# Eight single filling places per round of a RWKV-7 chunk loop, in place of four places with six parts

## The chip, the cores and the metric

The kernel runs on one core of one Trainium2 chip. The metric is device time in microseconds (us), from the start to the end of one execution; three timed runs of the kernel before gave a median of 1094.38 us (1093.92 to 1094.64).

The core has a matrix engine (TensorE, PE in the profile; its weight loads are listed apart as PEld), a vector engine (VectorE, DVE), an activation engine (ScalarE, ACT) and GpSimd (POOL). Each runs its own instructions in the order in which they are written, and they meet at semaphores. SyncE (SP) issues the loads of the weights.

## The reference, cut to what matters

One layer of a hybrid encoder: adaLN-modulated RMSNorm, one large projection, three token mixers on its slices (differential attention, HGRN2, RWKV-7), gated merging, then a SwiGLU channel mixer. 512 tokens, width 1024, all float32. The change lies in the RWKV-7 mixer, whose recurrence is

```python
def step(state, inp):
    r_t, w_t, k_t, v_t, kk_t, a_t = inp
    sa = jnp.einsum('bhvk,bhk->bhv', state, -kk_t)
    state = (state * w_t[:, :, None, :] + sa[..., None] * (kk_t * a_t)[:, :, None, :]
             + v_t[..., None] * k_t[:, :, None, :])
    return state, jnp.einsum('bhvk,bhk->bhv', state, r_t)
```

over 8 heads of 64 by 64 state. The columns of the projection that feed the gates, HGRN2 and the attention do not depend on this recurrence.

## The kernel before

**Chunks and pairs.** The recurrence is computed in chunks of 64 tokens, two chunks (`ab` 0 and 1) to a pair, four pairs (`PAIRS`). For a pair `n`, `start_inverse(n)` (line 2414) multiplies keys by queries (`AR`, `BK`), and VectorE masks the result into `SC` (`begin_inverse`, line 1749). Then the inverse of a unit triangular 64x64 matrix per head is built in five levels. Level `i` is a chain through three engines: `level_t(n, i)` (line 2424) is 16 products of 64x64 on TensorE (`SC` by `X`), `take_t` (line 1094) copies the result from its bank to `LX` on ScalarE, `level_p(n, i)` (line 2437) is 16 more products on TensorE (`XT` by `LX`), and on VectorE `level` (line 1774) writes the result into `X` under a mask and transposes it to `XT` for the next level's `level_p`. The next level's `level_t` needs only `X`. In the last level it is `XT` that is written.

**The state.** For each chunk of pair `c`, TensorE runs `read_values` and `read_state` (right-hand side, which ScalarE copies to `rhs_u`), `out_state`, `new_values` (the inverse applied; ScalarE copies it to `UV`), `write_state` (into `M`, which VectorE adds and decays in `next_state`, line 1790) and `out_chunk`.

**The rounds.** The loop at line 2558 runs three rounds, c = 0, 1, 2. A round interleaves the state's products of pair c with the inverse of pair c + 1, so that one chain's products stand between another's. The two transposes `values_by_token` (tile `V`) and `keys_by_token` (tile `BK`) stand there too.

**Filling.** Products of the large projection are put between the small ones. A weight panel has 256 columns and is computed as two units of 128 columns, and a unit as four parts; a part is six matmuls of 128x512 (three for each of two row blocks, since each float32 operand is split into a high and a low piece). `early(place)` on TensorE (line 2262) issues as many parts as the table `EARLY` (line 64) gives that place; the count of parts over the whole RWKV stretch is fixed by the later stages. In a round there are four places: `rw lo` (two parts, behind `start_inverse`), `rw mid` (one), `rw gap` (one) and `rw hi` (two), the last three around the last two levels. So a round takes six parts, three quarters of a panel.

**What follows a place.** The functions `early` of ScalarE (line 913) and VectorE (line 1505) carry the same place names. ScalarE's copies the units that are finished out of their bank to `gate_row` and sends them to memory, and splits off the high piece of the next panel (tile `whi`); VectorE's subtracts it from the panel to get the low piece (`wlo`). Which panel is due at a place follows from the count of parts ahead of it. Both stand in their engine's order between the steps of the inverse and of the state.

**Order.** All of it is written by hand: the order in which the functions are called is the order in each engine's queue. Results of small products use four memory banks in rotation (`bank_plan`, line 202), the units two more.

Of the kernel before, what the change touches and what calls it, by code (L numbers as in the profile page):

```python
# [45 lines left out]
PAIRS = T // P  # L46
# [15 lines left out]


EARLY = [
    [("rw lora", 4), ("rw kk", 4)] + [(("rw kn", x_), 4) for x_ in range(2)]
    + [(("rw sums", n, x_), 4) for n in range(3) for x_ in range(2)]
    + [("rw pro", 4)] + [((what, i), 1) for i in range(1, 4) for what in ("rw first", "rw lev")] + [(("rw lev", 4), 2)]
    + [((what, c), n) for c in range(PAIRS - 1) for what, n in (("rw lo", 2), ("rw mid", 1), ("rw gap", 1), ("rw hi", 2))]
    + [(("rw fin", k), n) for k, n in enumerate((1, 1, 4, 2, 2))]
    + [("rw mean", 4), ("rw bv", 2), ("rw var", 2), ("rw g", 8), ("rw past", 8), ("rw end", 0)],  # L70
    [(("hg z", 0), 4), (("hg z", 1), 4)] + [(("hg sc", lev), 2) for lev in range(1, LEVELS + 1)]
# [130 lines left out]
def bank_plan():  # L202
# [78 lines left out]
    for c in range(PAIRS):  # L281
        last = c == PAIRS - 1
        b.add("rw o", c, bank=4 + c % 2)
        if last:
            two("rw r", c, 0)
            b.add("rw u", c, 0)
            b.add("rw m", c, 0)
            two("rw r", c, 1)
            b.add("rw u", c, 1)
            for _ in range(2):  # L290
                late_ada(bank=4)
            continue
        inverse_start(c + 1)
        two("rw r", c, 0)
        b.add("rw t", c + 1, 1)
        b.add("rw u", c, 0)
        level(c + 1, 1)
        b.add("rw m", c, 0)
        two("rw r", c, 1)
        b.add("rw t", c + 1, 2)  # L300
        level(c + 1, 2)
        b.add("rw u", c, 1)
        b.add("rw t", c + 1, 3)
        b.add("rw m", c, 1)
        level(c + 1, 3)
        last_levels(c + 1)
    b.rotate(6)
# [80 lines left out]
def build(nc, x, ada_w, w_in, wba, wbb, wbc, w_out, f_in, f_out, w2, a2, g2,  # L388
# [3 lines left out]
    with ExitStack() as ctx:  # L392
# [495 lines left out]
        def _(act):  # L888
# [23 lines left out]

            def early(place):

                for part in early_parts()[:stretch(place)[1]]:
                    u = evicted[0]
                    if part[1] != u or not part[5]:
                        continue
                    evicted[0] += 1
                    act.wait_ge(*full("early", u))  # L920
                    if u >= 2:
                        act.wait_ge(*spilled(u - 2))
                    do(stage[:, u % 2, :], bank_of("early", u)[:, :], ACT.Copy).then_inc(free_sem("early", u), 1)  # L923
                    act.wait_ge(*freed("early", u))
                    act.dma_start(early_out[u], stage[:, u % 2, :]).then_inc(s_spilled[u % 2], 16)
                while split_next[0] < split_by(place):
                    split_hi()
# [152 lines left out]
            act.wait_ge(s_rw_bonus_hi, up(s_rw_bonus_hi))  # L1080
            for n in range(1, 3):
                for x_ in range(2):
                    early(("rw sums", n, x_))

# [56 lines left out]
            for c in range(PAIRS - 1):  # L1141
                if c == 2:

                    act.wait_ge(s_lam_dot, 2)
                    do(col(LR, 2), col(LR, 2), ACT.Exp).then_inc(s_lam_exp, 1)
                    act.wait_ge(s_lam_exp, up(s_lam_exp))
                early(("rw lo", c))
                take_r(c, 0)
                take_t(c + 1, 1)
                take_u(c, 0)  # L1150
                take_t(c + 1, 2)
                take_r(c, 1)
                take_u(c, 1)
                take_t(c + 1, 3)
                early(("rw mid", c))
                take_t(c + 1, 4)
                if c + 2 < PAIRS:
                    take_values(c + 2)
                take_o(c)
                early(("rw gap", c))  # L1160
                early(("rw hi", c))
                take_t(c + 1, 5)
                take_keys(c + 1, 0)
                if c + 2 < PAIRS:
                    take_keys(c + 1, 1)
            c = PAIRS - 1
            early(("rw fin", 0))
            take_r(c, 0)
            early(("rw fin", 1))
            take_u(c, 0)  # L1170
# [10 lines left out]
            early("rw bv")  # L1181
            early("rw var")
            act.wait_ge(*freed("rw mean", 3))
            do(chunks(epi), O, ACT.Square).then_inc(s_rw_sq, 1)
            act.wait_ge(s_rw_sq, up(s_rw_sq))
            for c in range(4):
# [238 lines left out]
        def _(dve):  # L1425
# [280 lines left out]
            for x_ in range(2):  # L1706
                early(("rw sums", 2, x_))
            dve.wait_ge(s_rw_factor, 1)
# [64 lines left out]

            def level(n, i, state=None):

                if i < RW_LEVELS - 1:
                    dve.wait_ge(*full("rw p", n, i))
                    v.copy_predicated(X[:, :, :], lmask(i, 0), by_chunk(bank_of("rw p", n, i)[:, :]))\  # L1778
                        .then_inc(free_sem("rw p", n, i), 1)
                    dve.wait_ge(*freed("rw p", n, i))  # L1780
                    if state is not None:
                        next_state(*state)
# [25 lines left out]
            for c in range(PAIRS - 1):  # L1808
# [3 lines left out]
                elif c == 1:  # L1812
# [3 lines left out]
                    for x_ in range(2):  # L1816
# [4 lines left out]
                        dve.wait_ge(s_lam_dot, up(s_lam_dot))  # L1821
                early(("rw lo", c))
                level(c + 1, 1, (c, 0))
                level(c + 1, 2)
                next_state(c, 1)
                level(c + 1, 3)
                early(("rw mid", c))
                level(c + 1, 4)
                early(("rw gap", c))
                early(("rw hi", c))  # L1830
                level(c + 1, 5)
# [3 lines left out]
            c = PAIRS - 1  # L1835
            early(("rw fin", 0))
            early(("rw fin", 1))
            next_state(c, 0)
# [320 lines left out]
        def _(pe):  # L2159
# [225 lines left out]
            pe.wait_ge(s_rw_norm_lo, 1)  # L2385
            for c in range(4):
                ps = begin("rw kn", c)
                mm(ps[:, :], select[:, P * c:P * c + P], norm_hi[:, :], True, False)
# [7 lines left out]
            end(last, "rw bonus")  # L2396
            for x_ in range(2):
                early(("rw sums", 1, x_))
            for x_ in range(2):
                early(("rw sums", 2, x_))  # L2400

# [129 lines left out]

            def last_levels(n, fourth, between, fifth):
# [5 lines left out]
                if between:  # L2538
                    early(between)
                level_p(n, 4)  # L2540
# [10 lines left out]
            for i in range(1, 4):  # L2551
# [3 lines left out]
                if i < 3:  # L2555
                    early(("rw lev", i))
            last_levels(0, ("rw lev", 3), None, ("rw lev", 4))
            for c in range(PAIRS - 1):
                start_inverse(c + 1)
                early(("rw lo", c))  # L2560
# [44 lines left out]
            early("rw bv")  # L2605
            for c in range(4):
                ps = begin("rw bv", c)
                mm(ps[:, :], select[:, P * c:P * c + P], bonus_hi[:, :], True, False)
# [280 lines left out]
```

## Time and profile before

| | |
|---|---|
| median of three timed runs | 1094.38 us |
| the profiled execution | 1092.74 us |
| its span, first to last instruction | 1090.9 us |
| TensorE busy | 1060.5 us (97%) |
| VectorE busy | 617.5 us (57%) |
| ScalarE busy | 455.0 us (42%) |
| mean granted clock of TensorE | 0.997 of full |

The span is 1.84 us shorter than the time of the same execution, which also holds what lies around the first and the last instruction. In the timeline a row merges neighbouring instructions of one kind: its columns are the start, the duration from the first start to the last end, the engine and line, what is written from what, the tile shape, the output shape and how many instructions there are. A small float32 product is listed twice (16 products are x32). A bracket gives the engine's idle time before the row and what ended it. Matmuls overlap at their ends, so the price of a group is taken from its start to the start of the next group.

### The profile page before, as it was taken

Reading aid. Unit: us, or ns where it says so; the run is one execution under the profiler, and the core shown is the slowest. Engines: PE = TensorE matmul, PEld = TensorE weight load, DVE = VectorE, ACT = ScalarE, POOL = GpSimd, SP = SyncE. Lnnn points to the kernel's source line nnn. Section 1 sums busy time; section 2 is a strip of 40 time slices with the busy share of each in tenths; the row PEclk is TensorE's granted clock in tenths of the full one; section 3 lists DMA queues with packets and bytes.
Section 4 is the critical chain, followed back from the end, with each engine's and each line's share of the span. In section 5 each row is a group of like instructions: output and inputs, shape, how many; then the busy total and the mean of one; then the engine's idle time right before and its main releaser. Section 6 shows DMA issues by size and latency. Waiting matters only on the chain.

```text
span 1090.9 us, 17055 instructions
## 1 busy us (share of the span) xinstructions
PE 1060.5 (97%) x7093; PEld 858.2 (79%) x7093; DVE 617.5 (57%) x846; ACT 455.0 (42%) x575; POOL 26.8 (2%) x46
## 2 busy tenths in 40 slices
PE   8999999999999999999999999999999999999997
PEld 6788677788887787787667778888888888878885
DVE  3489885467535469758656388663544533242446
ACT  5422743233323476655555454581222122222233
POOL 0100001000000000020000100000000000000000
PEclk9999999999999999999999999999999999999999
DMA  9977534301107421196411485304343423222201
GB/s 341 319 243 259 173 106 140 96 14 56 54 22 260 126 96 68 48 274 229 127 57 49 149 333 187 123 20 154 116 155 116 145 87 109 85 91 103 92 25 77
DMA packets 106772, 145.29 MB, mean 133 GB/s; under 512 B 3252, under 2 KB 86440, under 8 KB 106696
## 3 DMA queue, kind: packets, MB, share of 16 engines
q1 hardware_dynamic: 93544, 109.25, 30.4%
q0 software_dynamic: 5664, 21.32, 5.9%
q10 hardware_dynamic: 7488, 13.63, 3.3%
q8 instruction: 56, 0.92, 0.3%
q14 instruction: 20, 0.16, 0.0%
HBM read 128.46 MB, written 15.73 MB: 132 GB/s over the span
## 4 chain that ended last, share of the span: by engine, by line
PE 79%; DVE 11%; ACT 5%; DMA 2%; SPq 1%; issue 1%; ACTq 0%; POOL 0%; DVEq 0%
PE bank L2178 78%; DVE Z L1430 1%; DVE wlo L1430 1%; DVE q_lev L1430 1%; DMA raw<-in_w_in 1%; DMA qk<-early_out 1%; DVE near L1922 1%; SPq L794 1%; ACT whi L908 1%; DVE SC L1430 1%; DVE mg L1430 1%; ACT gate_row L923 1%; DVE ada_acc L1433 0%; DVE qk L1430 0%; PE bank L2735 0%
## 5 line engine op out<-in xcount | busy, mean ns | idle before, releaser
L2178 PE MATMUL bank<-hhi,whi 128*128 128x512 f32 (+1 forms) x800 | 318.6, 398 | 4.6 <-ACT gate_row L923 2.9
L2178 PE MATMUL bank<-hhi,wlo 128*128 128x512 f32 (+1 forms) x800 | 309.4, 387 | 0.0
L2178 PE MATMUL bank<-hlo,whi 128*128 128x512 f32 (+1 forms) x800 | 309.1, 386 | 0.0
L1430 DVE TENSOR_TENSOR wlo<-raw,whi 128x2048 fp32r<-128x2048 f32 (+1 forms) x80 | 166.3, 2079 | 246.7 <-ACT whi L908 241.2
L908 ACT ACTIVATE whi<-raw 128x2048 fp32r<-128x2048 f32 (+1 forms) x76 | 135.4, 1782 | 228.9 <-PE bank L2178 178.1
L2178 PEld LDWEIGHTS bank<-hhi,whi 128*128 128x128 f32 x800 | 150.6, 188 | 45.7 <-issue 10.2
L2178 PEld LDWEIGHTS bank<-hhi,wlo 128*128 128x128 f32 x800 | 150.6, 188 | 31.1
L2178 PEld LDWEIGHTS bank<-hlo,whi 128*128 128x128 f32 x800 | 150.8, 189 | 29.0 <-issue 0.7
L2178 PE MATMUL bank<-whi,d_hi 128*128 128x512 f32 x160 | 62.3, 390 | 1.2 <-DVE hid L1430 1.2
L2178 PE MATMUL bank<-whi,d_lo 128*128 128x512 f32 x160 | 62.3, 389 | 0.0
L2178 PE MATMUL bank<-wlo,d_hi 128*128 128x512 f32 x160 | 62.3, 389 | 0.0
L1397 ACT ACTIVATE f_tmp<-bank 128x512 f32<-128x512 f32 x22 | 13.2, 598 | 92.0 <-PE bank L2178 91.9
L923 ACT ACTIVATE gate_row<-bank 128x512 f32<-128x512 f32 x52 | 31.1, 598 | 29.1 <-PE bank L2178 27.0
L1433 DVE SCALAR_TENSOR_TENSOR ada_acc<-raw,ca,ada_acc 128x256 f32<-128x256 f32 x96 | 40.8, 480 | 0.6
L2178 PEld LDWEIGHTS bank<-whi,d_hi 128*128 128x128 f32 x160 | 30.0, 188 | 7.8 <-issue 1.6
L1097 ACT ACTIVATE LX<-bank 128x512 f32<-128x512 f32 x20 | 11.9, 597 | 58.1 <-PE bank L2178 58.1
L2178 PEld LDWEIGHTS bank<-whi,d_lo 128*128 128x128 f32 x160 | 30.0, 188 | 6.3
L2178 PEld LDWEIGHTS bank<-wlo,d_hi 128*128 128x128 f32 x160 | 30.0, 188 | 6.1
L1430 DVE TENSOR_TENSOR hid<-f_tmp,bank 128x512 f32<-128x512 f32 x22 | 15.1, 687 | 30.7 <-PE bank L2178 30.3
L1778 DVE COPY_PREDICATED X<-lev,bank 128x512 f32<-128x512 uint8 x16 | 11.7, 732 | 33.9 <-PE bank L2178 33.9
L2178 PE MATMUL bank<-whi,hhi 128*128 128x512 f32 x64 | 25.4, 397 | 0.0
L2178 PEld LDWEIGHTS bank<-X,SC 64*64 64x64 f32 x640 | 20.4, 134 | 5.9 <-issue 3.9
(367 smaller groups left out, 1537.3 us busy)
## 6 DMA issues: line engine op xcount, KB each, us to landing
raw<-in_w_in SPq DMA_DIRECT2D x33, 1024.0 KB, 5.6
raw<-in_f_in SPq DMA_DIRECT2D x22, 1024.0 KB, 4.9
raw<-in_ada_w SPq DMA_DIRECT2D x16, 1024.0 KB, 5.1
early_out<-gate_row ACTq DMA_DIRECT2D x52, 256.0 KB, 2.1
raw<-in_f_out SPq DMA_DIRECT2D x11, 1024.0 KB, 5.1
cond<-in_ada_w SPq DMA_DIRECT2D x8, 1024.0 KB, 10.7
sg<-early_out POOLq DMA_DIRECT2D x4, 1536.0 KB, 10.2
raw<-in_w_out SPq DMA_DIRECT2D x4, 1024.0 KB, 5.0
```

The source lines that it names most:

```text
L794: sp.dma_start(cond[f % COND][:, :, :], src).then_inc(s_cond_in[f], 16)
L908: do(hi_slots[slots[m]][:, 0:src.shape[1]], src, ACT.Copy).then_inc(s_panel_hi, 1)
L923: do(stage[:, u % 2, :], bank_of("early", u)[:, :], ACT.Copy).then_inc(free_sem("early", u), 1)
L1097: do(LX[:, :, :], by_chunk(bank_of("rw t", n, i)[:, :]), ACT.Copy).then_inc(free_sem("rw t", n, i), 1)
L1397: do(f_tmp[:, m, :], ps[:, :], ACT.Sigmoid).then_inc(s_ffn_sig, 1)
L1430: return v.tensor_tensor(out_, a, b, op)
L1433: return v.scalar_tensor_tensor(out=out_, in0=a, scalar=s_, in1=b, op0=op0, op1=op1)
L1778: v.copy_predicated(X[:, :, :], lmask(i, 0), by_chunk(bank_of("rw p", n, i)[:, :]))\
L1922: v.copy_predicated(near[:, 2 * half:2 * half + 2, :, :].rearrange("p c h t -> p (c h) t"), mask, by_chunk(bank_of("hg sc", lev, half)[:, ...
L2178: return t.matmul(out_, lhsT, rhs, start=start, stop=stop, skip_group_check=True)
```

## The change

The three rounds get eight places of one part each. In a round they now stand behind `start_inverse`, the first `out_state`, `level_t(n, 1)`, the second `read_values`, `level_t(n, 2)`, the second `out_chunk`, `level_p(n, 3)` and `level_p(n, 4)`; the first part of a round is the first of a panel, and a round takes one whole panel. Some calls change place with them: the first `new_values` goes ahead of `level_t(n, 1)`, the second `read_values` goes behind `level_p(n, 1)`, `level_t(n, 3)` goes behind the second `write_state` and `out_chunk`, and the two `keys_by_token` are divided between levels 4 and 5. On VectorE `next_state(c, 0)` goes ahead of level 1, and the panel's low piece is taken once per round, between levels 1 and 2. On ScalarE the copy of finished units and the split of a panel's high piece are separate (`evict` and `early`).

The six parts that the rounds gain are taken from ahead of the loop (24 parts in `rw sums` become 18, two go to a new place `rw kn mid` in the middle of four normalising products) and from behind it (`rw past` has six parts and not eight; two of the parts around the variance move to a new place `rw bv mid`). The count of the whole stretch stays 104.

The diff, cut to its core:

```diff
-    + [((what, c), n) for c in range(PAIRS - 1) for what, n in (("rw lo", 2), ("rw mid", 1), ("rw gap", 1), ("rw hi", 2))]
+    + [(("rw loop", c, k), 1) for c in range(PAIRS - 1) for k in range(LOOP_PLACES)]
...
             for c in range(PAIRS - 1):
-                start_inverse(c + 1)
-                early(("rw lo", c))
+                n = c + 1
+                start_inverse(n)
+                early(("rw loop", c, 0))
                 read_values(c, 0)
                 read_state(c, 0)
                 out_state(c, 0)
-                level_t(c + 1, 1)
+                early(("rw loop", c, 1))
                 new_values(c, 0)
-                level_p(c + 1, 1)
+                level_t(n, 1)
+                early(("rw loop", c, 2))
                 write_state(c, 0)
                 out_chunk(c, 0)
+                level_p(n, 1)
                 read_values(c, 1)
-                level_t(c + 1, 2)
+                early(("rw loop", c, 3))
                 read_state(c, 1)
                 out_state(c, 1)
-                level_p(c + 1, 2)
+                level_t(n, 2)
+                early(("rw loop", c, 4))
                 new_values(c, 1)
-                level_t(c + 1, 3)
+                level_p(n, 2)
                 write_state(c, 1)
                 out_chunk(c, 1)
-                level_p(c + 1, 3)
-                last_levels(c + 1, ("rw mid", c), ("rw gap", c), ("rw hi", c))
+                early(("rw loop", c, 5))
+                level_t(n, 3)
+                if n + 1 < PAIRS:
+                    values_by_token(n + 1)
+                level_p(n, 3)
+                early(("rw loop", c, 6))
+                level_t(n, 4)
+                keys_by_token(n, 0)
+                level_p(n, 4)
+                early(("rw loop", c, 7))
+                level_t(n, 5)
+                if n + 1 < PAIRS:
+                    keys_by_token(n, 1)
+                level_p(n, 5)
```

**Place one, TensorE, the middle of round c = 0, around `level_t(1, 3)`.** `X,SC` is the end of `level_t`, `LX,XT` is `level_p`, `UV,KBtok` and `SC,UV` are `write_state` and `out_chunk`, `cst,V` is `values_by_token`, and `hhi,whi` and the like are a part. Before:

```order
L2178 MATMUL bank<-X,SC_98 64x64
L2178 MATMUL bank<-X,SC_99 64x64
L2178 MATMUL bank<-UV_93,KBtok_101 64x64 x8
L2178 MATMUL bank<-SC_97,UV_93 64x64 x8
L2178 MATMUL bank<-LX,XT_91 64x64 x16
L2178 MATMUL bank<-hhi,whi 128x512
```

Now:

```order
L2183 MATMUL bank<-X,SC_98 64x64
L2183 MATMUL bank<-X,SC_99 64x64
L2416 MATMUL bank<-cst,V 128x128 x4
L2183 MATMUL bank<-LX,XT_91 64x64 x16
L2183 MATMUL bank<-hhi,whi 128x512
```

Between the two products of level 3 stood 16 products of the state; now there are the four transposes of `V`.

**Place two, TensorE, the end of the same round, around `level_t(1, 5)`.** `cst,BK` is `keys_by_token`, `XT,LX` is `level_p` of the last level, `AR,BK` is the next round's `start_inverse`. Before:

```order
L2178 MATMUL bank<-X,SC_98 64x64
L2178 MATMUL bank<-X,SC_99 64x64
L2459 MATMUL bank<-cst,BK 128x128 x8
L2178 MATMUL bank<-XT_91,LX 64x64 x16
L2178 MATMUL bank<-AR,BK 128x128 x16
```

Now:

```order
L2183 MATMUL bank<-X,SC_98 64x64
L2183 MATMUL bank<-X,SC_99 64x64
L2464 MATMUL bank<-cst,BK 128x128 x4
L2183 MATMUL bank<-XT_91,LX 64x64 x16
L2183 MATMUL bank<-AR,BK 128x128 x16
```

Half of the transposes that stood between the last level's two products has moved to level 4; in round c = 2 there are none there.

**Place three, TensorE, the start of the same round.** `UV,SC` is `read_values`, `M,AR` is `read_state`, `AR,M` is `out_state`, `rhs_u,XT` is `new_values`. Before:

```order
L2178 MATMUL bank<-UV_92,SC_96 64x64 x8
L2178 MATMUL bank<-M,AR 64x64 x8
L2178 MATMUL bank<-AR,M 64x64 x8
L2178 MATMUL bank<-X,SC_98 64x64
L2178 MATMUL bank<-X,SC_99 64x64
```

Now:

```order
L2183 MATMUL bank<-UV_92,SC_96 64x64 x8
L2183 MATMUL bank<-M,AR 64x64 x8
L2183 MATMUL bank<-AR,M 64x64 x8
L2183 MATMUL bank<-hhi,whi 128x512
L2183 MATMUL bank<-hlo,whi 128x512
L2183 MATMUL bank<-hhi,wlo 128x512
L2183 MATMUL bank<-hhi,whi 128x512
L2183 MATMUL bank<-hlo,whi 128x512
L2183 MATMUL bank<-hhi,wlo 128x512
L2183 MATMUL bank<-rhs_u,XT_90 64x64 x8
```

A part has come between `out_state` and the next small product, which is now `new_values` and no longer `level_t`.

## Rows read from the trace of the kernel before

**Rows 1.** The page, part 1: TensorE's and VectorE's busy time, share, instructions.

```profile
PE 1060.5 (97%) x7093; PEld 858.2 (79%) x7093; DVE 617.5 (57%) x846; ACT 455.0 (42%) x575; POOL 26.8 (2%) x46
```

**Rows 2.** Busy time by stretch: before the loop, rounds 0 to 2, behind it.

```profile
core 0: us, PE busy (x) PEld busy (x) DVE busy (x) ACT busy (x) POOL busy (x), PEclk, DMA share, GB/s
160.00:181.00 21.00, 21.00 (x86) 14.85 (x85) 13.18 (x9) 6.24 (x7) 0.00 (x0) 1.00 0.35 120
220.10:252.05 31.95, 31.20 (x597) 27.46 (x593) 20.96 (x32) 11.73 (x19) 1.04 (x2) 1.00 0.06 19
252.05:284.06 32.01, 31.21 (x596) 27.46 (x592) 18.67 (x33) 9.29 (x18) 1.04 (x2) 1.00 0.13 43
284.06:314.56 30.50, 30.39 (x589) 26.62 (x585) 15.87 (x22) 10.15 (x17) 0.00 (x0) 1.00 0.16 54
330.00:384.00 54.00, 54.00 (x238) 39.77 (x239) 26.38 (x33) 22.63 (x23) 2.25 (x3) 1.00 0.58 193
```

**Rows 3.** Timeline of TensorE, end of round 0: single and double parts, transposes.

```profile
240.21 0.50 PE L2178 MATMUL bank<-hhi,whi 128*128 128x512 f32 x1
...
241.79 1.15 PE L2178 MATMUL bank<-X,SC 64*64 64x64 f32 x32
242.87 0.66 PE L2411 MATMUL bank<-cst,V 128*128 128x128 f32 x4
243.28 0.47 PE L2178 MATMUL bank<-hhi,whi 128*128 128x512 f32 x1
...
245.92 0.50 PE L2178 MATMUL bank<-hhi,whi 128*128 128x512 f32 x1
...
248.87 1.15 PE L2178 MATMUL bank<-X,SC 64*64 64x64 f32 x32
249.95 1.09 PE L2459 MATMUL bank<-cst,BK 128*128 128x128 f32 x8
250.97 1.15 PE L2178 MATMUL bank<-XT,LX 64*64 64x64 f32 x32
```

**Rows 4.** Timeline of TensorE: the waits at `level_t(n, 2)` in rounds 0 and 1.

```profile
233.03 1.09 PE L2178 MATMUL bank<-X,SC 64*64 64x64 f32 x30 [0.75 <-DVE X L1778]
...
265.04 1.09 PE L2178 MATMUL bank<-X,SC 64*64 64x64 f32 x30 [0.80 <-DVE X L1778]
```

**Rows 5.** Timeline of TensorE: `read_state`/`out_state`, before a small product and before a part.

```profile
226.28 0.51 PE L2178 MATMUL bank<-M,AR 64*64 64x64 f32 x10
...
227.16 0.27 PE L2178 MATMUL bank<-X,SC 64*64 64x64 f32 x1
...
315.63 0.51 PE L2178 MATMUL bank<-M,AR 64*64 64x64 f32 x10
...
316.71 0.50 PE L2178 MATMUL bank<-hhi,whi 128*128 128x512 f32 x1
```

**Rows 6.** Timeline of TensorE: `level_t` to `level_p` with little between them.

```profile
210.99 1.15 PE L2178 MATMUL bank<-X,SC 64*64 64x64 f32 x32
...
212.89 0.27 PE L2178 MATMUL bank<-LX,XT 64*64 64x64 f32 x2 [0.17 <-ACT LX L1097]
...
311.63 1.15 PE L2178 MATMUL bank<-X,SC 64*64 64x64 f32 x32
312.71 0.65 PE L2459 MATMUL bank<-cst,BK 128*128 128x128 f32 x4
313.48 1.15 PE L2178 MATMUL bank<-XT,LX 64*64 64x64 f32 x32
```

**Rows 7.** Timelines of ScalarE, VectorE and TensorE, ahead of pair 0's inverse.

```profile
175.49 0.60 ACT L923 ACTIVATE gate_row<-bank 128x512 f32<-128x512 f32 x1 [4.79 <-PE bank L2178]
...
178.60 2.29 DVE L1430 TENSOR_TENSOR wlo<-raw,whi 128x2048 fp32r<-128x2048 f32 x1 [2.44 <-ACT whi L908]
181.01 0.27 DVE L1710 MEMSET M<- 128x256 f32 x1
...
186.18 0.60 PE L2411 MATMUL bank<-cst,V 128*128 128x128 f32 x4
```

**Rows 8.** Timelines of VectorE and ScalarE, behind the loop.

```profile
376.13 2.29 DVE L1430 TENSOR_TENSOR wlo<-raw,whi 128x2048 fp32r<-128x2048 f32 x1 [5.54 <-ACT whi L908]
...
411.15 0.60 ACT L923 ACTIVATE gate_row<-bank 128x512 f32<-128x512 f32 x1 [1.54 <-PE bank L2178]
```

More of the change, by code:

```diff
@@ L292, in bank_plan @@
             continue
-        inverse_start(c + 1)
+        n = c + 1
+        inverse_start(n)
         two("rw r", c, 0)
-        b.add("rw t", c + 1, 1)
         b.add("rw u", c, 0)
-        level(c + 1, 1)
+        b.add("rw t", n, 1)
         b.add("rw m", c, 0)
+        level(n, 1)
         two("rw r", c, 1)
-        b.add("rw t", c + 1, 2)
-        level(c + 1, 2)
+        b.add("rw t", n, 2)
         b.add("rw u", c, 1)
-        b.add("rw t", c + 1, 3)
+        level(n, 2)
         b.add("rw m", c, 1)
-        level(c + 1, 3)
-        last_levels(c + 1)
+        b.add("rw t", n, 3)
+        if n + 1 < PAIRS:
+            b.add("rw v", n + 1)
+        level(n, 3)
+        b.add("rw t", n, 4)
+        b.add("rw kb", n, 0)
+        level(n, 4)
+        b.add("rw t", n, 5)
+        if n + 1 < PAIRS:
+            b.add("rw kb", n, 1)
+        level(n, 5)
     b.rotate(6)
@@ L911, in _, with evict @@
             evicted = [0]
-            def early(place):
+            def evict(place):
                 for part in early_parts()[:stretch(place)[1]]:
@@ L925, in early @@
                     act.dma_start(early_out[u], stage[:, u % 2, :]).then_inc(s_spilled[u % 2], 16)
+            def early(place):
+                evict(place)
                 while split_next[0] < split_by(place):
@@ L1080, in _ @@
             act.wait_ge(s_rw_bonus_hi, up(s_rw_bonus_hi))
-            for n in range(1, 3):
-                for x_ in range(2):
-                    early(("rw sums", n, x_))
+            for n, x_ in ((1, 0), (1, 1), (2, 0)):
+                early(("rw sums", n, x_))
             def take_values(n):
@@ L1146, in _ @@
                     act.wait_ge(s_lam_exp, up(s_lam_exp))
-                early(("rw lo", c))
+                n = c + 1
+                evict(("rw loop", c, 0))
                 take_r(c, 0)
-                take_t(c + 1, 1)
                 take_u(c, 0)
-                take_t(c + 1, 2)
+                take_t(n, 1)
+                early(("rw loop", c, 2))
                 take_r(c, 1)
+                take_t(n, 2)
+                evict(("rw loop", c, 4))
                 take_u(c, 1)
[L1154 to L1158, printed above, removed]
-                take_o(c)
[L1160 to L1165, printed above, removed]
+                take_o(c)
+                take_t(n, 3)
+                if n + 1 < PAIRS:
+                    take_values(n + 1)
+                take_t(n, 4)
+                take_keys(n, 0)
+                take_t(n, 5)
+                if n + 1 < PAIRS:
+                    take_keys(n, 1)
             c = PAIRS - 1
-            early(("rw fin", 0))
+            evict(("rw fin", 0))
             take_r(c, 0)
-            early(("rw fin", 1))
             take_u(c, 0)
@@ L1705, in _ @@
                     dve.wait_ge(s_dve_step, up(s_dve_step))
-            for x_ in range(2):
-                early(("rw sums", 2, x_))
+            early(("rw sums", 2, 0))
             dve.wait_ge(s_rw_factor, 1)
@@ L1772, in transpose_x, with level @@
                 dve.wait_ge(s_rw_xt, up(s_rw_xt))
-            def level(n, i, state=None):
+            def level(n, i):
                 if i < RW_LEVELS - 1:
@@ L1780, in level @@
                     dve.wait_ge(*freed("rw p", n, i))
-                    if state is not None:
-                        next_state(*state)
                     transpose_x(n)
@@ L1821, in _ @@
                         dve.wait_ge(s_lam_dot, up(s_lam_dot))
-                early(("rw lo", c))
-                level(c + 1, 1, (c, 0))
+                next_state(c, 0)
+                level(c + 1, 1)
+                early(("rw loop", c, 2))
                 level(c + 1, 2)
@@ L2386, in _ @@
             for c in range(4):
+                if c == 2:
+                    early("rw kn mid")
                 ps = begin("rw kn", c)
@@ L2396, in _ @@
             end(last, "rw bonus")
[L2397 to L2400, printed above, removed]
+            for n, x_ in ((1, 0), (1, 1), (2, 0)):
+                early(("rw sums", n, x_))
             def rows64(tile, g, hl, chunk):
@@ L2530, in write_state, with last_levels @@
                 end(last, "rw m", c, ab)
-            def last_levels(n, fourth, between, fifth):
+            def last_levels(n, fourth, fifth):
                 early(fourth)
@@ L2606, in _ @@
             for c in range(4):
+                if c == 2:
+                    early("rw bv mid")
                 ps = begin("rw bv", c)
```

21 lines of the change are left out of this document (9 added, 12 removed).

## The prediction

> **What bounds the kernel now.** I read the page first: TensorE is busy for 1060.5 of 1090.9 us [rows 1], so what a change can win by ordering is the idle time of TensorE where it acts, and what it can lose is time that TensorE spends between instructions. Then the busy time by stretch [rows 2]: the three rounds last 31.95, 32.01 and 30.50 us, and in them TensorE is idle for 0.75, 0.80 and 0.11 us. Ahead of the loop (160 to 181) and behind it (330 to 384) it is never idle. The reader is to see there that all that filling could win in the rounds is under 1.7 us, 0.15% of the time. Rows 4 show where it lies: `level_t` of level 2 waits for VectorE's `X`, once in each of the first two rounds. Then the timeline of TensorE, for the price of a joint between a part and a small product [rows 3, 5], and for the time from `level_t` to `level_p` when little stands between them [rows 6].
>
> **The moved parts.** Two parts in a run, from 245.92 to the small product at 248.87, take 2.95 us; one, from 240.21 to 241.79, takes 1.58 [rows 3]. So a part costs 1.37 us, and every run of parts, long or short, 0.21 more. The rounds get six more parts, 6 x 1.37 = 8.2 us. As many are taken out of stretches where TensorE is never idle [rows 2], so the parts by themselves cancel.
>
> **More runs.** A round had four runs of parts and has eight: 3 x 4 = 12 more. The two new places in the normalising products and in the variance cut runs in two as well: 14 in all, 14 x 0.21 = 2.9 us. This is measured in the same form, so I hold it to within 0.7.
>
> The Trainium skill, TensorEngine Tiling (Array Packing), Key Properties, speaks against the change here: changing the tiling mode, not just the tile, drains TensorE, and a part (128x128) between 64x64 products changes it twice. Its page TensorE: Matmul & The Clock Gate, Single matmul latency, puts the drain at about 175 ns plus the columns; two per run would be 0.35 us, an estimate from that page, and 4.9 us for 14 runs in place of 2.9. The row's 0.21 decides, since it holds both changes.
>
> **Small products parted.** From `read_state` to a following small product it is 0.88 us (226.28 to 227.16), to a following part 1.08 (315.63 to 316.71) [rows 5]: small products of one shape run into each other, and lose 0.20 when a part comes between. A new part cuts four such joints per round (behind `out_state`, `level_t` 1, `read_values` and `level_t` 2). The first costs 0.20; the others I bound between 0 and 0.20 each, and take 0.25 together, since not all have the same tile shape. 0.45 a round, 1.35 us; bounds 0.6 and 2.4.
>
> **The old waits.** With a part and `read_state` and `out_state` between `level_p` 1 and `level_t` 2, VectorE has over 3 us for `X`. The waits of 0.75 and 0.80 [rows 4] go: -1.55 us. The range for this term is -1.55 to 0.
>
> **New waits.** This is the largest term. `level_p` needs ScalarE's copy of what `level_t` made. Where only transposes stand between the two, the time from start to start was 1.90 us (210.99 to 212.89, where the row gives ScalarE's `LX` as the releaser) and 1.85 (311.63 to 313.48, with four transposes of `BK`) [rows 6]. I take 1.87 as the least time from one to the other, whatever stands between. `level_t` alone takes 1.08, four transposes of `V` 0.41, and eight of `BK` 1.02, so four 0.51 [rows 3]. Before, a part, 16 + 16 state products or eight transposes covered the copy in nearly all places. Now:
> - level 3, four transposes of `V`: 1.87 - 1.08 - 0.41 = 0.38;
> - level 4, four of `BK`: 1.87 - 1.08 - 0.51 = 0.28;
> - level 5, four of `BK`: 0.28.
>
> That is 0.94 in rounds 0 and 1. In round 2 there is no `V` and no second `BK`: levels 3 and 5 have nothing between, 0.79 each, and level 4 has 0.28. Of that 0.26 was there before (the 1.85 of rows 6 is this round's level 5), so 1.60 is new. Together 2 x 0.94 + 1.60 = 3.5 us. From below it is 0, if something hides the copy that I don't see; from above 5, if ScalarE is in the midst of another 0.6 us copy at some of these places.
>
> **The wait for M.** Four parts fewer stand ahead of pair 0's transposes of `V`, which need the zeroed state. TensorE would come there at 186.18 - 4 x 1.37 = 180.7. The chain to the zeroing stays where it was: unit finished and copied at 175.49, panel split on ScalarE, low piece 178.60 to 180.89, zeroing until 181.28 [rows 7]. So TensorE waits 0.6 us; bounds 0 and 0.9.
>
> **What is moved and costs nothing.** A panel's split (ScalarE's high piece, then VectorE's low piece of 2.29 us [rows 7]) now stands between levels 1 and 2 once a round. On VectorE level 2 is queued behind it, and its `level_p` comes some 8 us after that of level 1 by the prices above. On ScalarE the copies of the second right-hand side are behind it, some 6 us later. VectorE is busy 21 us of a round of 32 [rows 2]. If the cover failed, it would cost up to 2.29 a round. Behind the loop, the norm's chain comes two parts, 2.7 us, later beside the count of parts; VectorE then stands still for 5.54 us waiting for a panel that hangs on that count alone [rows 8], so that chain catches up. Without that idle time it would be 2.7 us. The HGRN2 stage starts when ScalarE gets a unit for which it waited 1.54 us on TensorE [rows 8]: whatever TensorE loses up to there is passed on to the end in full. The queue of loads on SP keeps its order; its waits are for panels taken, which are taken no later.
>
> **The sum.** 2.9 + 1.35 - 1.55 + 3.5 + 0.6 = +6.8 us. The rounds become 31.95 + 2.74 + 0.84 + 0.45 - 0.75 + 0.94 = 36.2, the same for the second, and 30.50 + 2.74 + 0.84 + 0.45 + 1.60 = 36.1 for the third. The profiled execution took 1092.74 us and would take 1099.5; it lies 1.6 below the median of the three timed runs, 1094.38, so the median would be 1101.2.
>
> **The rivals.**
> - *The copies stay hidden.* ScalarE's copy may come sooner than in rows 6, or the small products behind it may be held anyway. Then 3.5 falls away: +3.3, 1097.7. For it: only two rows show the 1.87. Against it: both agree to 0.05, and one names the copy.
> - *The split in the wrong place.* If `level_p` 2 comes sooner behind level 1 than VectorE's two steps and the 2.29 us of the low piece, or if ScalarE's half is late, the chain of the inverse waits in each round: up to 3 x 2.29 = 6.9 more, 1108. For it: rows 7 show TensorE's work hanging on just such a split. Against it: the 8 us above.
> - *Not slower.* TensorE's weight loads are busy 27.46 of 31.95 us in a round, 86%, against 39.77 of 54.00, 74%, among parts alone [rows 2]. If the small products are held by their weight loads, a part ahead of them lets TensorE load in its shadow, and each group behind a part becomes shorter. Five groups a round stand newly behind a part; if each drops from 1.08 to the 0.88 of rows 5, that gives 15 x 0.20 = 3.0. With the copies hidden too, 6.8 - 3.0 - 3.5 = +0.3, 1094.7. It decides from a gain of 0.3 per group on (15 x 0.3 = 4.5, or 4.5 + 3.5 with hidden copies, against 6.8). Against it: `level_t` behind one part and behind two takes 1.08 both times (241.79 to 242.87, 248.87 to 249.95), and no group behind a part was shorter [rows 3].
> - *The clock* stays at 1.00, the 2.4 GHz level, in all three rounds [rows 2], waits of 0.8 included; the new waits are no longer than those. I give its fall no share of its own.
>
> **How the numbers follow.** My forecast has 0.74, with 1099.5 to 1103.0 as its own range from the terms' bounds. The hidden copies have 0.10, the misplaced split 0.08, the last rival 0.08. About 0.2%, 2.2 us, is what a measurement of this kernel can tell from no change; the first three lie above that, and of the last I give 0.06 to within it and 0.02 to faster. So slower 0.92, same 0.06, faster 0.02. The range of 8 in 10 takes in the forecast, the hidden copies and the milder half of the misplaced split: 1097.0 to 1104.0.
>
> **What would show it.** The rounds at 36 us; in them no wait at `level_t` 2; waits of TensorE on ScalarE's `LX` at `level_p` of levels 3, 4 and 5, longest in the last round, with 1.85 to 1.9 from start to start; a part alone 1.58 from its start to the next; TensorE waiting about half a microsecond for `M` before pair 0. If `level_p` 3 comes closer than 1.8 us behind `level_t` 3, the new waits are wrong. If VectorE's `wlo` is the releaser inside a round, the split is misplaced. If groups behind a part take 0.9 or less, the last rival holds. If the rounds are 36 us and the end is not later by 6 to 7, something behind the loop took the loss up, and the reading of rows 8 is wrong.

## The result, and the profile after

The changed kernel takes 1104.52 us (median of five runs, 1103.41 to 1105.27) against 1094.38 for the kernel before (1093.25 to 1095.08, five runs on the same chip): ratio 1.0097, interval 1.0085 to 1.0108, some 10 us slower. The forecast was 1101.2, with a range of 1097.0 to 1104.0. The sign is right; the size is not, and the time lies just outside the range. The profiled execution of the changed kernel took 1104.52 us, its span is 1102.7. Two runs of the kernel before beside the experiments below (1510.71 and 1183.19 us, at a mean granted clock of 0.65 and 0.85) stay out of the ratios, while the medians contain them.

First the page's busy times and TensorE's waits by releaser (us in total, times, longest), those in and around the RWKV stretch:

```profile
PE 1066.6 (97%) x7093; PEld 856.8 (78%) x7093; DVE 617.3 (56%) x846; ACT 455.6 (41%) x575; POOL 28.9 (3%) x46
```

```profile
PE bank L2183 <- DVE gate_row L1442: 3.3, 1, 3.3
...
PE bank L2183 <- ACT LX L1110: 2.7, 9, 0.8
```

Against [rows 1], TensorE is busy for 6.1 us more with the same 7093 matmuls. The wait for VectorE's `X` of [rows 4] is gone from the list. Nine waits for ScalarE's `LX` have come, as forecast, and one that no step of the prediction has: 3.3 us for a `gate_row` of VectorE's.

Busy time by stretch (columns as in [rows 2]): the three rounds, then the end of the RWKV stretch from the first part of `rw fin 3`.

```profile
214.55:250.86 36.31, 35.80 (x609) 29.55 (x605) 21.00 (x32) 12.23 (x20) 1.04 (x2) 1.00 0.14 46
250.86:287.17 36.31, 35.80 (x609) 29.56 (x605) 20.97 (x34) 11.76 (x21) 1.04 (x2) 1.00 0.14 46
287.17:323.48 36.31, 34.62 (x601) 28.72 (x597) 15.88 (x22) 10.37 (x17) 0.00 (x0) 1.00 0.14 45
338.78:346.25 7.47, 7.47 (x45) 5.73 (x42) 2.26 (x6) 3.89 (x6) 0.00 (x0) 1.00 0.95 322
346.25:349.55 3.30, 0.00 (x1) 0.03 (x1) 2.72 (x2) 0.27 (x1) 0.00 (x0) 1.00 0.15 57
349.55:351.42 1.87, 1.87 (x18) 1.20 (x18) 0.42 (x1) 0.00 (x0) 0.00 (x0) 0.58 0.65 135
351.42:357.83 6.41, 6.41 (x26) 5.25 (x25) 0.00 (x0) 3.54 (x4) 1.51 (x2) 0.86 1.02 320
357.83:369.42 11.59, 11.59 (x41) 7.18 (x40) 5.86 (x9) 4.43 (x3) 0.08 (x1) 1.00 0.31 119
```

The rounds are 36.31 us long (forecast 36.2, 36.2, 36.1). The surprise lies behind them. The same work of the kernel before, cut at the same instructions:

```profile
329.85:337.16 7.31, 7.31 (x46) 5.92 (x43) 4.20 (x11) 1.64 (x4) 0.00 (x0) 1.00 1.02 351
337.16:338.30 1.14, 1.14 (x20) 0.74 (x18) 0.42 (x1) 0.00 (x0) 0.00 (x0) 1.00 0.64 248
338.30:343.91 5.61, 5.61 (x28) 4.61 (x25) 0.00 (x0) 4.92 (x5) 1.50 (x2) 1.00 0.55 187
343.91:355.06 11.15, 11.15 (x41) 7.34 (x40) 7.80 (x9) 3.05 (x3) 0.75 (x1) 1.00 0.68 238
```

From `rw fin 3` to the mean it was 7.31 + 1.14 + 5.61 = 14.06 us. It is 7.47 + 3.30 + 1.87 + 6.41 = 19.05, so 5.0 more for the same products: 3.30 of idle time, 1.5 in the two stretches behind it, where the granted clock is 0.58 and 0.86 of full in place of 1.00, and 0.16 in the stretch ahead of it, whose cause was not sought.

What TensorE waited for is read from the timelines of ScalarE, VectorE and TensorE of the changed kernel:

```profile
342.92 0.59 ACT L1132 ACTIVATE UV<-bank 64x512 f32<-64x512 f32 x1 [3.02 <-PE bank L2183]
343.55 0.60 ACT L933 ACTIVATE gate_row<-bank 128x512 f32<-128x512 f32 x1
344.18 0.33 ACTq L935 DMA_DIRECT2D early_out<-gate_row  x1
344.60 1.92 ACT L918 ACTIVATE whi<-raw 128x2048 fp32r<-128x2048 f32 x1 [0.46 <-ACT gate_row L933]
```

```profile
346.65 2.29 DVE L1442 TENSOR_TENSOR wlo<-raw,whi 128x2048 fp32r<-128x2048 f32 x1 [5.54 <-ACT whi L918]
348.98 0.42 DVE L1442 TENSOR_TENSOR gate_row<-bank,gate_row 128x256 f32<-128x256 f32 x1
```

```profile
342.82 0.70 PE L2183 MATMUL bank<-ada_acc,cst 128*128 128x256 f32 x2
343.16 0.58 PE L2183 MATMUL bank<-hhi,whi 128*128 128x512 f32 x1
...
349.55 0.89 PE L2183 MATMUL bank<-ada_acc,cst 128*128 128x256 f32 x2 [3.30 <-DVE gate_row L1442]
```

TensorE makes two late adaLN products (`ada_acc,cst`, one on either side of the two parts of `rw fin 4`) in one and the same bank. VectorE empties it into `gate_row`, and the second product waits until the first is taken out. In the kernel before VectorE did that at once:

```profile
334.68 0.42 DVE L1430 TENSOR_TENSOR gate_row<-bank,gate_row 128x256 f32<-128x256 f32 x1 [0.95 <-PE bank L2178]
337.84 0.42 DVE L1430 TENSOR_TENSOR gate_row<-bank,gate_row 128x256 f32<-128x256 f32 x1 [2.74 <-PE bank L2178]
344.58 2.29 DVE L1430 TENSOR_TENSOR wlo<-raw,whi 128x2048 fp32r<-128x2048 f32 x1 [6.31 <-ACT whi L908]
```

Now the low piece of a panel (`wlo`) stands ahead of it in VectorE's queue, and waits itself for ScalarE's high piece (`whi`), which stands behind the copies of `UV` and of a unit. The chain from 342.92 is 0.59 + 0.60 + 0.45 of issue + 1.92 + 2.29 + 0.42 with its joints, 6.6 us, and TensorE has only the two parts, 3.1 us, to spend meanwhile.

Nothing in the diff is written at this place. What moved is a count. With the places of `EARLY` added up, 70 parts stood ahead of `rw fin 0` and 72 do now. A panel is eight parts, so part 80 (counted from 0), the first of the panel that starts there, moved from `rw mean` into `rw fin 4`. The split of the next panel falls due where a new one is begun, so it moved with it: from `early("rw mean")`, behind the two `ada_out` steps on VectorE, to `early(("rw fin", 4))`, ahead of them.

### The profile page after: what moved, and what is told of

It reads as the page before. It is cut to its first block, busy times and chain, and to the rows that moved or that the text cites. A ratio compares the mean times of both kernels' runs of the same rounds, so it can differ in the third digit from the quotient of the medians.

```text
span 1102.7 us, 17051 instructions
## 1 busy us (share of the span) xinstructions
PE 1066.6 (97%) x7093; PEld 856.8 (78%) x7093; DVE 617.3 (56%) x846; ACT 455.6 (41%) x575; POOL 28.9 (3%) x46
## 4 chain that ended last, share of the span: by engine, by line
PE 80%; DVE 9%; ACT 6%; DMA 2%; SPq 1%; issue 1%; ACTq 0%; POOL 0%; DVEq 0%
PE bank L2183 79%; DVE wlo L1442 1%; DVE Z L1442 1%; DVE q_lev L1442 1%; DMA raw<-in_w_in 1%; DMA qk<-early_out 1%; ACT whi L918 1%; DVE near L1927 1%; SPq L804 1%; ACT gate_row L933 1%; ACT LX L1110 1%; DVE mg L1442 1%; DVE ada_acc L1445 0%; DVE qk L1442 0%; PE bank L2756 0%
## 5 line engine op out<-in xcount | busy, mean ns | idle before, releaser
L1789 DVE COPY_PREDICATED X<-lev,bank 128x512 f32<-128x512 uint8 x16 | 11.8, 736 | 48.2 <-PE bank L2183 48.2
L2183 PE MATMUL bank<-wlo,hhi 128*128 128x512 f32 x64 | 24.9, 389 | 0.0
```

What stands on the lines that cost most here:

```text
L2183: return t.matmul(out_, lhsT, rhs, start=start, stop=stop, skip_group_check=True)
```

## The experiments

None of these kernels leaves out any work. Times are medians; "the trace" is one profiled execution. The comparisons with the kernel before were made on the same chip: its median was 1093.56 us beside the first two kernels and the last two, 1093.97 beside the four between. Where stages are summed, the stretch goes from the first normalising product of RWKV to the first product of HGRN2: 236.1 us in the kernel before, 248.9 after.

**The two `ada_out` first.** VectorE's queue alone is changed:

```diff
             early(("rw fin", 3))
-            early(("rw fin", 4))
             for k in range(2):
                 ada_out(ADA[18 + k])
+            early(("rw fin", 4))
             early("rw mean")
```

> The changed kernel with one step moved: on VectorE the call for the place rw fin 4, at which the low piece of a panel is now due, goes behind the two steps that empty the bank of the late adaLN products, not ahead of them. Theory (a panel's split has come to stand ahead of the emptying of that bank, TensorE waited 3.30 us for it and then ran at a granted clock of 0.58 and 0.86): the wait is gone, the clock stays at 1.00, the stretch from the last parts ahead of new_values to the mean products takes 14.1 us as before the change and not 19.1, so 5.0 us less than the changed kernel, about 1099.5. Rival (the delay only moves on, since the low piece of 2.29 us now stands ahead of the mean's steps on VectorE): the wait appears further on and the time falls by 1 us or less, about 1104.

Measured: 1099.6 us, ratio 1.0058 (1.0044 to 1.0072). In the trace the stretch from `rw fin 3` to the mean is as before, with no idle time and the full clock:

```profile
340.40:354.46 14.06, 14.06 (x87) 11.27 (x85) 5.40 (x9) 7.71 (x10) 1.50 (x2) 1.00 0.77 256
```

VectorE's timeline shows the two steps at once again, and the low piece behind them:

```profile
345.23 0.42 DVE L1442 TENSOR_TENSOR gate_row<-bank,gate_row 128x256 f32<-128x256 f32 x1 [2.50 <-PE bank L2183]
348.40 0.42 DVE L1442 TENSOR_TENSOR gate_row<-bank,gate_row 128x256 f32<-128x256 f32 x1 [2.74 <-PE bank L2183]
348.86 2.29 DVE L1442 TENSOR_TENSOR wlo<-raw,whi 128x2048 fp32r<-128x2048 f32 x1
```

So the order of these two steps on VectorE is the cause of the missing 5.0 us in the trace. What is left is the change as the prediction had seen it, and it lies inside the range that was forecast.

**The old rounds with the new counts.** The kernel above, with the old order of the small products inside a round and its four runs of parts, each now of two (the panel's split behind level 3 on VectorE). The diff is cut to the places of the parts; ScalarE's and VectorE's steps are in the old order too:

```diff
                 start_inverse(n)
                 early(("rw loop", c, 0))
+                early(("rw loop", c, 1))
...
                 level_p(n, 3)
+                early(("rw loop", c, 2))
+                early(("rw loop", c, 3))
                 level_t(n, 4)
...
+                early(("rw loop", c, 4))
+                early(("rw loop", c, 5))
                 level_p(n, 4)
                 early(("rw loop", c, 6))
                 early(("rw loop", c, 7))
                 level_t(n, 5)
```

> As e1, and inside the rounds the old order of the small products and four runs of parts, now two parts each, so eight parts a round still. Theory (it is the order and the number of runs that lengthen the rounds, the two more parts of a round are only moved): rounds of 34.7, 34.7 and 33.2 us in place of 36.3 each, 6.2 us less than e1, about 1093 to 1096 and within 0.2% of the kernel before. Rival (moving parts into the rounds costs by itself, because what is taken out elsewhere is not saved): rounds as said, but a time 2 us or more above the kernel before, about 1097 to 1100.

Measured: 1093.58 us, ratio 1.0001 (0.9992 to 1.0009). The rounds last 34.69, 34.73 and 33.28, which is 2.74, 2.72 and 2.78 above [rows 2]: two parts of 1.37 each and next to nothing else. So longer runs cost just their parts, and the eight single places and the new order cost 36.31 - 34.69 = 1.62 us in the first round, 1.58 in the second and 3.03 in the last, which had no wait for `X` to lose and has two levels with nothing to cover the copy. TensorE's timeline shows the old waits back:

```profile
228.83 1.09 PE L2175 MATMUL bank<-X,SC 64*64 64x64 f32 x30 [0.76 <-DVE X L1780]
263.57 1.09 PE L2175 MATMUL bank<-X,SC 64*64 64x64 f32 x30 [0.80 <-DVE X L1780]
```

**The old rounds, panel first.** The same with the `early(("rw fin", 4))` of VectorE left where the change has it, ahead of the two `ada_out`:

```diff
+            early(("rw fin", 4))
             for k in range(2):
                 ada_out(ADA[18 + k])
-            early(("rw fin", 4))
```

> As e3 (old order inside the rounds, two parts at each of four runs), but with the panel's low piece on VectorE at rw fin 4 ahead of the emptying of the late adaLN bank again, as in the changed kernel. Theory (the count of parts alone puts a panel's split at that place, whatever the rounds look like): the wait of 3.3 us of TensorE is there, the granted clock falls behind it, the time is 5.0 us above e3, about 1098.6. Rival (the wait needs the later arrival that the new rounds bring): no wait over 1 us there, the time of e3, 1093.6.

Measured: 1099.16 us, ratio 1.0039 (1.0024 to 1.0055). The wait is there without any of the new rounds; the trace's stretch is 5.0 us longer than that of the kernel with the old rounds. TensorE's timeline, and the busy time behind the wait:

```profile
344.72 0.96 PE L2175 MATMUL bank<-ada_acc,cst 128*128 128x256 f32 x2 [3.30 <-DVE gate_row L1433]
```

```profile
344.72:349.00 4.28, 4.28 (x25) 3.12 (x26) 0.42 (x1) 2.13 (x3) 1.50 (x2) 0.60 0.82 255
```

In time the wait is worth 0.38% here (1.0039 against 1.0001) and 0.39% in the new rounds (1.0097 against 1.0058), some 4.2 us. That lies between the 3.3 of idle time alone and the 5.0 with the lost clock, and the intervals are too wide to choose.

**The copies covered.** The first kernel with two groups put elsewhere: the second `write_state` and `out_chunk` go back between the products of level 3, and the transposes of `V` go beside those of `BK` in level 4. ScalarE's copies change their order with them (`take_t` of level 3 goes ahead of `take_o`, that of level 4 ahead of `take_values`), which the cut leaves out:

```diff
                 level_p(n, 2)
-                write_state(c, 1)
-                out_chunk(c, 1)
                 early(("rw loop", c, 5))
                 level_t(n, 3)
-                if n + 1 < PAIRS:
-                    values_by_token(n + 1)
+                write_state(c, 1)
+                out_chunk(c, 1)
                 level_p(n, 3)
                 early(("rw loop", c, 6))
                 level_t(n, 4)
+                if n + 1 < PAIRS:
+                    values_by_token(n + 1)
                 keys_by_token(n, 0)
```

> As e1, with other work moved back between level_t and level_p: the second write_state and out_chunk between those of level 3, and the transposes of V beside those of the keys at level 4. Eight single places stay. Theory (the waits at level_p are ScalarE's copy, 1.87 us from level_t to level_p at least): the waits at levels 3 are gone in all rounds, those at level 4 in rounds 0 and 1, while level 5 keeps 0.28, 0.28 and 0.79; rounds of about 35.6, 35.6 and 35.5 us in place of 36.3, 2.1 us less than e1. Rival (the waits only move to the other side, to level_t of the next level, since VectorE's X has less ahead of it): rounds of 36.1 or more.

Measured: 1097.86 us, ratio 1.0035 (1.0025 to 1.0045). The rounds last 35.67, 35.68 and 35.46, together 2.1 us less than in the first kernel. Of the nine waits for `LX`, four are left:

```profile
PE bank L2183 <- ACT LX L1110: 1.3, 4, 0.8
```

TensorE's timeline in its round 0 shows the limit of 1.90 us at level 5 and its absence at level 4, where eight transposes (`V` and `BK`) now stand between the two products:

```profile
244.68 1.15 PE L2183 MATMUL bank<-X,SC 64*64 64x64 f32 x32
245.75 0.66 PE L2416 MATMUL bank<-cst,V 128*128 128x128 f32 x4
246.25 0.60 PE L2464 MATMUL bank<-cst,BK 128*128 128x128 f32 x4
246.78 1.15 PE L2183 MATMUL bank<-LX,XT 64*64 64x64 f32 x32
249.44 1.15 PE L2183 MATMUL bank<-X,SC 64*64 64x64 f32 x32
250.52 0.66 PE L2464 MATMUL bank<-cst,BK 128*128 128x128 f32 x4
251.34 1.15 PE L2183 MATMUL bank<-XT,LX 64*64 64x64 f32 x32 [0.17 <-ACT LX L1110]
```

Level 4 goes from 244.68 to 246.78 in 2.10 us with no wait, level 5 from 249.44 to 251.34 in 1.90 with one. So the new waits are what the prediction took them for, and they can be covered by order alone (here TensorE's and ScalarE's together).

**The zeroing first.** The first kernel, with VectorE's zeroing of `M` ahead of the panel's low piece:

```diff
-            early(("rw sums", 2, 0))
             dve.wait_ge(s_rw_factor, 1)
...
             dve.wait_ge(s_rw_state, up(s_rw_state))
+            early(("rw sums", 2, 0))
```

> As e1, with the zeroing of M on VectorE ahead of the low piece of the panel, not behind it. Theory: TensorE's wait of 0.44 us for M ahead of pair 0's transposes is gone, and the stretch from the bonus products to those transposes is 0.6 us shorter (20.0 in place of 20.6 us); nothing else changes. Rival (TensorE then waits for something else there, the transposed products' bank or the keys): a wait stays, 20.4 us or more.

Measured: 1098.82 us in one run. The wait for `M`, which the changed kernel's timeline of TensorE shows, is gone:

```profile
180.62 0.66 PE L2416 MATMUL bank<-cst,V 128*128 128x128 f32 x4 [0.44 <-DVE M L1721]
```

From the first product of the bonus to pair 0's transposes of `V` it takes 19.98 us and not 20.59, so the wait had cost 0.61. ScalarE's `UV` next door still makes TensorE wait for 0.36, as in the changed kernel.

**`rw lo` in two runs.** The kernel before, with the two parts of `rw lo` in a round parted, the second behind the first `out_state`:

```diff
                 out_state(c, 0)
+                early(("rw lo b", c))
                 level_t(c + 1, 1)
```

> The kernel before with one part of the two behind start_inverse moved behind the first out_state: one run of parts more in each round, nothing else. Theory (a run costs 0.21 us of its own, and 0.20 more where it parts out_state from level_t): each round 0.4 us longer, 32.35, 32.4 and 30.9 us, unless the part behind out_state also takes away some of the wait of 0.75 at level_t of level 2, which hangs on VectorE and would then shrink by as much in rounds 0 and 1; round 2, which has no such wait, shows the plain price. Rival (a run costs nothing by itself): round 2 unchanged at 30.5.

Measured: 1095.65 us in one run. Round 2, which has no wait for `X`, grows from 30.50 to 30.86: 0.36 for one run more and the joint that it parts. Rounds 0 and 1 stay at 31.94 and 32.00, since the wait for `X` shrinks from the 0.75 of [rows 4] by the same amount:

```profile
233.18 1.09 PE L2178 MATMUL bank<-X,SC 64*64 64x64 f32 x30 [0.38 <-DVE X L1778]
```

The time of this run prices nothing, because in its trace the granted clock falls twice outside the rounds while TensorE is never idle, which lengthens the normalising products (14.74 for 13.15 us) and the variance (12.47 for 11.15):

```profile
146.00:152.00 6.00, 6.00 (x21) 4.33 (x20) 3.45 (x5) 5.44 (x5) 0.00 (x0) 0.77 0.71 218
354.00:358.00 4.00, 4.00 (x10) 2.75 (x9) 0.36 (x1) 0.00 (x0) 0.75 (x1) 0.57 0.38 112
```

**The angles moved.** The kernel before with one thing changed: VectorE's steps for the rotary angles, which stood at the start of rounds 0 and 1 ahead of the levels, are done in pair 0's inverse and behind the rounds.

```diff
                 begin_inverse(c + 1)
-                if c == 0:
-                    angles(1)
-                elif c == 1:
-                    angles(0)
...
                 level(0, i)
+                if i == 1:
+                    angles_first(1)
+                elif i == 2:
+                    angles_rest(1)
...
             early(("rw fin", 1))
+            angles_first(0)
+            angles_rest(0)
             next_state(c, 0)
```

> The kernel before, with VectorE's steps on the rotary angles moved out of rounds 0 and 1: one set into the idle time of VectorE in pair 0's levels, the other behind the rounds. Theory (the old waits of 0.75 and 0.80 us at level_t of level 2 came from these steps, which hold up X): both waits are gone, rounds of 31.2 us, 1.5 us less, about 1092.9. Rival (the waits come from the chain of the level itself, next_state between X and its transposition): waits of 0.7 to 0.8 remain, time unchanged, 1094.4.

Measured: 1092.11 us, ratio 0.9987 (0.9976 to 0.9999). The rounds last 31.14 and 31.16 us (31.95 and 32.01 in [rows 2]), and no wait for `X` is left. That is what filling the rounds could win at most, without one part more in them, and the fastest of the kernels here, though its interval all but touches no change.

**The kernel before, again.**

> The kernel before, unchanged, profiled a second time. Theory (the profiled execution of before was a short one because of what lies ahead of the RWKV stretch, where the loads decide): the rounds and the stretches behind them agree with the first profile to 0.1 us, and the start of the normalising products moves by 1 us or so. Rival (the stretches of the change themselves vary from run to run): they differ by more than 0.5 us.

Measured: 1093.61 us, ratio 1.0006 (0.9994 to 1.0018). Its rounds agree with [rows 2] to 0.02 us, as the theory has it. But one stretch of the change itself varied, as the rival has it: the whole came out at 237.7 us, 1.6 longer than in the first trace, all of it between the normalising products and the bonus, where the granted clock shows:

```profile
146.00:152.00 6.00, 6.00 (x25) 4.42 (x24) 5.47 (x6) 5.76 (x5) 0.00 (x0) 0.95 0.54 159
152.00:158.00 6.00, 6.00 (x21) 4.80 (x21) 3.51 (x3) 2.12 (x2) 0.00 (x0) 0.76 0.28 103
```

TensorE was busy throughout, and its last wait of any length, 0.51 us, lay 17 us back. So one trace holds a difference of 1 to 2 us in a stretch only where the clock is 1.00 in both.

## Why the prediction was wrong, point by point

Between the first normalising product and HGRN2 the stages of the first experiment, which has all of the change but the one wait, add up to 7.8 us over the kernel before, where the sum said 6.8. The changed kernel itself has 12.8.

- **The step that failed** is "What is moved and costs nothing". It checked the split of a panel inside the rounds, and behind the loop only the norm's chain. It did not follow the count of parts to each later place and ask which panel falls due there. The two parts more ahead of `rw fin 0` moved the split of one panel by one place, past two steps that empty a bank for TensorE, and TensorE stood still for 3.30 us. Cost: 5.0 us in the trace, some 4.2 in time. The rival "The split in the wrong place" had the mechanism, with VectorE's low piece ahead of what TensorE waits for, but sought it in the rounds. There it doesn't occur: no round shows `wlo` as a releaser.
- **The clock.** "I give its fall no share of its own" held for the waits that were foreseen: with waits of 0.17 to 0.76 the rounds stand at 1.00. It fails for the wait that was not. In both traces with 3.30 us of idle time the clock was down right behind it (0.58, then 0.86; 0.60).
- **The old waits** went, as forecast.
- **The new waits** were right in mechanism and nearly in size. All nine go from start to start in 1.90 us, not 1.87. Level 3 in a round with `V` and in round 2 without it, TensorE's timeline after:

```profile
238.73 1.15 PE L2183 MATMUL bank<-X,SC 64*64 64x64 f32 x32
239.81 0.65 PE L2416 MATMUL bank<-cst,V 128*128 128x128 f32 x4
240.63 1.15 PE L2183 MATMUL bank<-LX,XT 64*64 64x64 f32 x32 [0.17 <-ACT LX L1110]
...
311.35 1.15 PE L2183 MATMUL bank<-X,SC 64*64 64x64 f32 x32
313.25 1.15 PE L2183 MATMUL bank<-LX,XT 64*64 64x64 f32 x32 [0.76 <-ACT LX L1110]
```

  By the prediction's own subtraction that makes 1.03 a round for 0.94, and 1.69 for 1.60 in the last. The rival of the hidden copies falls.
- **More runs and parted products.** 1.62 us a round, less 1.03 of new waits, plus 0.75 of old ones, leaves 1.34 for four runs and the four joints in the first round; the last, with no old wait, gives 3.03 - 1.69 = 1.34 as well. The prediction had 0.84 + 0.45 = 1.29. How it divides between the two was not measured. Outside the rounds the term was mis-sized: the cut in the normalising products (13.15 to 13.59 us) and the one in the variance (11.15 to 11.59) cost 0.44 each, not 0.21. Each parts small products of one shape too, and the joint, up to 0.20 by [rows 5], was charged in the rounds and forgotten here; the two together make 0.41, but no run parts them. The estimate of 0.35 a run, worked out from the drain of the Trainium skill (TensorE: Matmul & The Clock Gate, Single matmul latency), was set beside the 0.21 alone. If it is taken to hold the parted joint as well, the traces come near it: 1.34 / 4 = 0.33 in the rounds, 0.36 in the kernel with `rw lo` in two runs, 0.44 in the cuts.
- **The wait for `M`** is 0.44 us of idle time, 0.61 from start to start; forecast 0.6.
- **The rest of the rows.** "Not slower" falls: `level_t` behind a part still takes 1.08 us. The norm's chain behind the loop caught up, as [rows 8] said: from the variance on, two parts fewer make 25.95 us of 28.64. What TensorE lost was passed on to the end: 12.8 us here, less 1.2 by which this execution came earlier to the first normalising product, is about the 11.8 by which the span grew.

So the sum of what was looked at was 1.0 short: 0.4 in the three rounds, 0.5 in the two cuts. That the forecast lies 1.6 above the 1099.6 us of the first experiment all the same is luck and no merit of the sum: 0.8 is the other base (1094.38 for the forecast, 1093.56 beside the experiment), and the 1.0 that the sum is short is more than made up by the 1.8 by which the trace exceeds the medians (7.8 against 1099.6 - 1093.56 = 6.0). The one wait carried the time past the range.

**What stays open.** The traces show 1 to 3 us more than the times do: 7.8 against 0.58% (6.3 us) in the first experiment, 1.6 against nothing in the old rounds, 12.8 against 10.1 here. The first trace of the kernel before had no fall of the clock in this stretch and the second had one of 1.6 us, and the first execution lies 1.6 below its kernel's median; so it may be a short one to compare with. The mean granted clock of each timed run, which is on record, points the same way. Three runs of the first experiment at 0.998 average 1099.4 us, and three of the kernel before at 0.998 average 1091.6: 7.8 apart, as in the trace. Four of the old rounds at 0.998 average 1092.9, 1.4 above and near the trace's 1.6. But 20 of the 26 runs of the kernel before that the ratios take in stood at 0.997 or lower, one of five in the first experiment and five of eleven in the old rounds, so the medians compare different clocks. The groups are small: this supports the reading and does not prove it. Nor is it shown that the idle time causes the fall behind it: it came in both traces with the wait and right at its end, and in none of the other eight at this place, but falls as deep (0.57 over 4 us in the trace of `rw lo` in two runs) came elsewhere without one.

## What to carry to other kernels

Where a table of counts decides when a large step falls due, a change of the counts can move it at every later place. List the due step of each place before and after, and look at what stands behind it in the same engine's queue, above all at whatever empties a bank that the matrix engine writes again. A small product put between two others costs its joints and takes away the cover that hid a copy; ask first whether the wait to be filled can be removed at its source, by moving off the engine that is late a step that nobody waits for.

## What the hardware showed that was not expected

- The granted clock fell to 0.58 and 0.60 of full (the 1.2 GHz level for most of the stretch, where full is 2.4) right behind 3.30 us of idle time, and stayed at 1.00 in rounds with waits of up to 0.80 us. It also fell to 0.76 over 6 us in one trace of the kernel before and to 0.77 over 6 us and 0.57 over 4 us in that of `rw lo` in two runs, with TensorE busy throughout.
- A run of parts that breaks a group of small products of one shape costs 0.33 (the rest of a sum) to 0.44 us; parts that lengthen a run cost next to nothing beside themselves, 2.72 to 2.78 us for two.
- From `level_t` to `level_p`, through ScalarE's copy, 1.85 us was the least in both kernels, in places where the row names no wait [rows 6], and each of the nine new waits makes it 1.90, whether nothing, four transposes of `V` or four of `BK` stand between; eight transposes hide it.
